# A two-block layer: gate sums of the matrix LSTM in nine matmuls, and the opening's loads in another order

## What is computed

```python
def _mlstm_feats(u, ib, fb):
    q, k, v, o, gates = _split_at(u, (ML_W, ML_W, ML_W, ML_W, 4 * ML_H))
    gates = gates.astype(jnp.float32).reshape(B, T, 2, 2, ML_H)
    ig = jnp.moveaxis(gates[:, :, :, 0] + ib, 1, -1)
    lf = jnp.moveaxis(jax.nn.log_sigmoid(gates[:, :, :, 1] + fb), 1, -1)
    return heads(q), heads(k) * ML_DH ** -0.5, heads(v), o, ig, lf

def _mlstm_scan(state, k, v, ig, lf, q, emit):
    b = jnp.cumsum(fc, axis=-1)
    dlog = jnp.where(tri, b[..., :, None] - b[..., None, :] + ic[..., None, :], -jnp.inf)
```

## Time and profile before

| | |
|---|---|
| median of 3 runs | 4479.27 us (4473.22 to 4482.85) |
| profiled execution | 4480.07 us, span 4478.3 us, mean granted TensorE clock 0.939 |
| TensorE (PE) busy | 4073.0 us, 91% |
| VectorE (DVE), ScalarE (ACT) busy | 2167.1 us, 1351.3 us |
| chain that ended last | PE 79%, DVE 12%, ACT 4%, issue 3%, DMA 1% |

### The profile page before, as it was taken

How to read it: one execution, slowest core, us unless ns; L and a number is a source line. 1 busy time by engine, 2 the same in 40 slices (tenths; PEclk the granted TensorE clock), 3 DMA queues, 4 the chain that set the end, 5 groups by cost and what they waited for, 6 DMA issues and landing times.

```text
span 4478.3 us, 70218 instructions
## 1 busy us (share of the span) xinstructions
PE 4073.0 (91%) x30400; PEld 3249.6 (73%) x30400; DVE 2167.1 (48%) x2920; ACT 1351.3 (30%) x1913; POOL 156.9 (4%) x197
## 2 busy tenths in 40 slices
PE   7987968877999999999978899999999987899998
PEld 4755768874767887888666578887888666578887
DVE  4756467753334445335555453335334646444335
ACT  4144243312324223222322432223222312433222
POOL 0000012220000000000000000000000001000000
PEclk8898979987999999999988899999999988889999
DMA  6111000015342223333200123332333100113331
GB/s 233 47 38 47 10 2 3 3 50 190 107 139 79 94 94 94 94 95 93 67 3 22 45 62 107 91 99 86 98 94 104 58 11 23 45 48 108 85 94 66
DMA packets 319381, 328.42 MB, mean 73 GB/s; under 512 B 10080, under 2 KB 243600, under 8 KB 318048
## 3 DMA queue, kind: packets, MB, share of 16 engines
q1 hardware_dynamic: 312144, 287.53, 20.9%
q0 software_dynamic: 6928, 36.40, 2.2%
HBM read 315.51 MB, written 8.39 MB: 72 GB/s over the span
## 4 chain that ended last, share of the span: by engine, by line
PE 79%; DVE 12%; ACT 4%; issue 3%; DMA 1%; POOL 0%; DVEq 0%; ACTq 0%; SPq 0%; POOLq 0%
PE psum L246 78%; DVE ring L300 3%; DVE ring L331 2%; DVE arena L300 2%; PE psum L253 2%; DVE arena L311 1%; ACT arena L350 1%; ACT ring L350 1%; DMA ring<-in_w_ada 1%; ACT r L350 1%; DVE r L300 1%; DVE arena L307 1%; DVE arena L305 0%; DVE arena L331 0%; DVE arena L319 0%
## 5 line engine op out<-in xcount | busy, mean ns | idle before, releaser
L246 PE MATMUL psum<-r 128*128 128x512 f32 (+2 forms) x13008 | 2928.7, 387 | 87.3 <-DVE r L300 70.4
L246 PEld LDWEIGHTS psum<-r 128*128 128x128 f32 x13008 | 2370.3, 189 | 636.3 <-issue 62.4
L300 DVE TENSOR_TENSOR r<-ring,r 128x2048 fp32r<-128x2048 f32 (+2 forms) x261 | 574.9, 2203 | 404.2 <-ACT r L350 399.7
L350 ACT ACTIVATE r<-ring 128x2048 fp32r<-128x2048 f32 (+2 forms) x261 | 479.2, 1836 | 401.5 <-PE psum L246 341.6
L350 ACT ACTIVATE arena<-psum 128x512 f32<-128x512 f32 (+6 forms) x472 | 258.9, 549 | 1125.1 <-PE psum L246 1045.8
L246 PE MATMUL psum<-arena 64*64 64x64 f32 (+18 forms) x2420 | 405.3, 335 | 56.0 <-DVE arena L300 29.8
L246 PE MATMUL psum<-ring 64*64 64x64 f32 (+4 forms) x8608 | 350.6, 236 | 86.2 <-ACT ring L350 34.5
L300 DVE TENSOR_TENSOR arena<-arena,psum 128x512 f32<-128x512 f32 (+4 forms) x220 | 129.9, 590 | 612.5 <-PE psum L246 559.5
L246 PEld LDWEIGHTS psum<-arena 128*128 128x128 f32 (+9 forms) x2420 | 261.2, 182 | 188.2 <-issue 112.9
L246 PEld LDWEIGHTS psum<-ring 64*64 64x64 f32 (+3 forms) x8608 | 289.6, 145 | 127.9 <-issue 48.3
L311 DVE SCALAR_TENSOR_TENSOR arena<-arena 128x512 f32<-128x512 f32 (+4 forms) x316 | 266.7, 844 | 117.9 <-ACT arena L350 107.0
(11 more groups left out here) (92 smaller groups left out, 1387.4 us busy)
## 6 DMA issues: line engine op xcount, KB each, us to landing
ring<-in_ffa_w_in SPq DMA_DIRECT2D x88, 512.0 KB, 5.2
ring<-in_ffb_w_in SPq DMA_DIRECT2D x88, 512.0 KB, 5.2
ring<-in_w_mlp SPq DMA_DIRECT2D x32, 1024.0 KB, 5.2
ring<-in_w_in SPq DMA_DIRECT2D x31, 1024.0 KB, 5.5
ring<-in_w_ada SPq DMA_DIRECT2D x24, 1024.0 KB, 5.5
ring<-in_mix_w_in SPq DMA_DIRECT2D x24, 1024.0 KB, 5.2
ring<-in_ffa_w_out SPq DMA_DIRECT2D x20, 1024.0 KB, 5.0
ring<-in_ffb_w_out SPq DMA_DIRECT2D x20, 1024.0 KB, 5.0
```

What stands on the lines that cost most here:

```text
L246: ins = self.raw.matmul(o, l, r, start=start, stop=stop, skip_group_check=True)
L300: self.done(self.raw and self.raw.tensor_tensor(o, a, b, f), keys)
L350: self.done(self.raw and self.raw.activation(o, i, f, scale=scale, bias=bias), keys)
```

## The change

Two things are changed. First, GpSimd waits, behind the four x tiles, until the sixth w_ada slab has been used, and only then issues ctx and the large constant tables. The norms of the two ctx tiles, on ScalarE and VectorE, move from the middle of the modulation rows to the end of the opening. Second, the sums of the gates are taken for all six tiles at once (nine matmuls: eight of 24 columns, one of 48), ahead of the rows; tiles that a direction doesn't need are computed too. VectorE makes the bias ahead of the rows, with 26 operations where there were 18, since the two neighbours that one copy read lie apart now.

```diff
@@ pool_first
         g.load(xtile(K, i), K.I["x"][0, 128 * i:128 * i + 128, :], "x", i)
+    g.wait_ge(*K.at("mod rows", 1, 0))
     for i in range(2):
         g.load(xtile(K, 4 + i), K.I["ctx"][0, 128 * i:128 * i + 128, :], "x", 4 + i)
     g.load(m.cst[:, 128:], K.I["consts"][:, 128:], "consts")
@@ act_first
     act_mod_rows(mod, K, 0, 1)
-    for i in (4, 5):
-        squares(i)
     act_mod_rows(mod, K, 1, 0, last=0)
...
         act_turned(a, K, "n1", 512, 0, f)
+    for i in (4, 5):
+        squares(i)
@@ dve_first
     dve_mod_rows(mod, K, 0, 1)
-    for i in (4, 5):
-        norm(i)
-    v.set(m.z[3], 0.0)
     dve_mod_rows(mod, K, 1, 0)
...
         dve_turned(v, K, "n1", 512, 0, f)
+    for i in (4, 5):
+        norm(i)
+    v.set(m.z[3], 0.0)
@@ pe_ml_rows
     t.wait_ge(*K.at("ml LF"))
+    o = t.take("ml sums")
+    for d in range(2):
+        lf, ig = m.LF[:, :, d, :], m.IG[:, :, d, :]
+        for x, mat in enumerate((C["LS128"], C["nUI128"]) if d == 0 else (C["US128"], C["nLI128"])):
+            p = view(o[:, 48 * d + 24 * x:48 * d + 24 * x + 24], [4, 6], [1, 4])
+            t.mm(p, mat, lf, True, False)
+            t.mm(p, C["ident"], ig, False, True)
+    t.mm(o[:, 96:144], C["ones"], view(m.LF, [1, 48]), True, True, ("ml sums",))
     for d in range(2):
         for x, X in enumerate((m.LF, m.IG)):
...
-    o = t.take("ml sums")
-    for d in range(2):
-        for x, tile in enumerate(SEQ_[d]):
-            lf, ig, c = m.LF[:, tile, d, :], m.IG[:, tile, d, :], 72 * d
-            if x < 5:
-                p = o[:, c + 8 * x:c + 8 * x + 4]
-                t.mm(p, C["LS128" if d == 0 else "US128"], lf, True, False)
-                t.mm(p, C["ident"], ig, False, True)
-            if 0 < x < 5:
-                t.mm(o[:, c + 44 + 4 * x:c + 48 + 4 * x], C["ones"], lf, True, True)
-            if x > 1:
-                p = o[:, c + 8 * x - 4:c + 8 * x]
-                t.mm(p, C["nUI128" if d == 0 else "nLI128"], lf, True, False)
-                t.mm(p, C["ident"], ig, False, True, ("ml sums",))
@@ dve_ml_in
     taps(conv, 9)
+    dve_ml_bias(v, K)
     dve_ml_rows(v, K)
     E.ahead()
-    dve_ml_bias(v, K)
     taps(conv, 18)
@@ dve_ml_bias
-        c, first = 72 * d, 18 * d
-        v.copy(m.bias[:, first, :], pv[:, c:c + 4])
-        last = first
+        P, D, T = ([pv[:, c + n * x:c + n * x + 4] for x in SEQ_[d]] for c, n in ((48 * d, 4), (48 * d + 24, 4), (96 + 4 * d, 8)))
+        last = first = 18 * d
+        v.copy(m.bias[:, first, :], P[0])
         for x in range(2, 6):
-            o = m.bias[:, first:first + x - 1, :]
-            v.tt(o, m.bias[:, last:last + x - 1, :], view(pv[:, c + 40 + 4 * x:c + 44 + 4 * x], [0, x - 1], [1, 4]), ADD)
-            v.copy(m.bias[:, first + x - 1:first + x + 1, :], view(pv[:, c + 8 * x - 8:c + 8 * x], [4, 2], [1, 4]),
-                   ("ml bias sb",))
+            v.tt(m.bias[:, first:first + x - 1, :], m.bias[:, last:last + x - 1, :], view(T[x - 1], [0, x - 1], [1, 4]), ADD)
+            v.copy(m.bias[:, first + x - 1, :], P[x - 1])
+            v.copy(m.bias[:, first + x, :], D[x], ("ml bias sb",))
             last, first = first, first + x + 1
```

## The result

The changed kernel takes 4443.45 us (median of 4 runs, 4441.4 to 4445.02) against 4476.25 us for the kernel before, timed beside it (4 runs): a ratio of 0.9925, 95% interval 0.9908 to 0.9943. Timed again in two later sessions it gave 4446.79 (ratio 0.993, 0.9918 to 0.9943) and 4446.95 us (0.9929, 0.9911 to 0.9948). The profiled execution took 4445.02 us with a span of 4443.2, against 4480.07 and 4478.3: 35.05 us less.

What follows compares the result with a forecast made beforehand. TensorE, busy 91% of the span, was taken as the bound, waiting for w_ada slabs and a bank held behind the sums. 8 us (9 - 1) plus 20.8 off 4479.3 gave 4451, range 4443 to 4463.

Steps and rivals of the forecast that it cites:

- w_ada first, 9 us (TensorE through at 35): Opening: with ctx and tables held back, TensorE finishes w_ada at 35 instead of 43.93, 9 us earlier (8 to 10).
- w_in's first split at 43, with two us of cover left: Opening: first w_in slab lands near 41; ScalarE splits it at 43 instead of 52.14, leaving two us to spare.
- Rival A: Opening: slab 7 or w_in's first slab waits out the 3.4 MB; the w_ada gain becomes 0, time 4458; chance 0.13.
- The rule of the Trainium skill: DMA queues: an engine drains a packet of each queue in turn, so large packets take the bandwidth.
- the argument against part one: Opening: w_in's first slab, in smaller pieces, crawls while tables run; the jam moves from slabs 3 to 5 onto slab 7 and w_in.
- Squares, 1.0 us: Opening: ctx's moved squares delay the split of w_in's second slab, costing 1.0 us (0 to 2).
- Sums, 1.8 us, and 3.5 idle: Matrix LSTM: nine products take 1.8 us instead of 15.17; TensorE then idles some 3.5 us before the eighth row group.
- k and v, 9.9 + 13.9 = 23.8 us: Matrix LSTM: k features take 9.9 us, then v's 60 matmuls 13.9 at 2.4 GHz, without a wait between.
- Rival B, the clock: Matrix LSTM: low clock lasts through k and v keeps 16.48 us; gain 10.8 instead of 20.8, time 4460; chance 0.11.
- C: Stages from 280 us on: clock falls come elsewhere and the kernel gets slower, 4488; chance 0.04.
- D: Matrix LSTM: VectorE with its 124 taps is the bound and TensorE waits there, so nothing arrives; about 4477; chance 0.04.
- The sum of 28.8 us: Total gain: 8 us from the opening plus 20.8 from the gate sums through the v features.

Runs made afterwards that it cites:

- What part two left: Changed kernel with the nine sums matmuls behind the eight row groups again and VectorE's bias between row copies and scans: 4442.97 us, ratio 0.9931.

## Why the prediction was right or wrong

The forecast was 4451, the time 4443.45: inside the range (4443 to 4463) by half a us, some 7 us below the likeliest, and outside the forecast's own bounds (4444 to 4461). The gain up to the first exponential was forecast rightly, in nearly all of its terms; the step from there to the time of the whole kernel failed.

- **w_ada first, 9 us (TensorE through at 35).** 34.25, 9.7 us. Slabs 2 and 3 were used at 17.0 and 19.7 (landing expected at 16.4 and 19.0), slab 5 done at 27.
- **w_in's first split at 43, with two us of cover left.** It came at 43.12, by two errors that cancel, which is luck. The turn of part 1 ran at the higher clock, so ScalarE was ready at 41.2; and the slab came at 43.1, not at 41. The traffic's length was about right (9 us, 8.4 forecast), its place was not: ctx was issued at 27.36, but GpSimd's queue moved nothing of it until 31, and was through at 40 where 38 was forecast. The cover wasn't left over but overspent by 1.95 us. Rival A was there, then, in small, and the tables' traffic was its cause, as the run that held them longer shows. What the lateness costs depends on ScalarE: in "What part two left", with the same opening, the turn ran at the low clock, ScalarE was ready later, and the wait was 0.23 us for a split at 43.02.
- **The rule of the Trainium skill (DMA: Bandwidth & Descriptors, on arbitration).** The trace agrees, if the profile's pieces are taken for the packets of that rule. In the changed kernel the queues moved, from 30 to 31, 33 to 34 and 35 to 40 us:

```profile
q1 hardware_dynamic: 350, 0.37, 110.1%
...
q0 software_dynamic: 84, 0.32, 79.0%
q1 hardware_dynamic: 84, 0.09, 24.2%
...
q0 software_dynamic: 115, 2.07, 97.4%
q1 hardware_dynamic: 115, 0.12, 6.8%
```

  Alone, SyncE's queue moves 350 pieces of w_in in 1 us. Beside ctx (pieces of 4 KB) it moves one of its 1 KB pieces for each of ctx's, and beside the tables (18 KB) too: 0.12 MB in 5 us, 5% of the bytes. So w_in did crawl, as the argument against part one had it. What it left out is the price. The crawl ends with the tables, at 40, and w_in was wanted only at 41.2, so 1.95 us of waiting were all that it cost.
- **Squares, 1.0 us.** 0.58 us of idle TensorE in the profile, and that wait is gone when the splits go first.
- **Sums, 1.8 us, and 3.5 idle.** 6.57 us for the sums and seven row groups against 1.8 + 4.6; idle 3.43. The bias took from 163.67 to the first row copy at 168.8, 26 operations at the forecast 0.197 us each.
- **k and v, 9.9 + 13.9 = 23.8 us.** 24.08, and 22.62 to 24.86 in other profiles of the same kernel.
- **Rival B, the clock.** It did fall between the rows and k, in four of the five profiles with the sums ahead of the rows (k and v in 24.08 to 24.86 us, against 22.62 in the fifth), but for 3 to 5 us of the k features and not for the whole of k and v. **C and D** got nothing: VectorE's taps were never waited for.

The sum of 28.8 us was measured as 28.71 at the first exponential (8.35 for the forecast 8, and 20.36 for 20.8). **What failed is the step behind it.** The prediction puts the stages from there on at nothing ("what is won there should be kept") and allows 4 us for them ("medians wander by 4 more"). They took 6.4 us less in the changed kernel's profile than in that of before, and 9.2 us less in one profile of before than in the other, with no edit between. The base was off as well: the 4479.27 from which I counted was the median of three, where four runs gave 4476.25 and later medians of before were 4475 to 4478. Of the 7 us that the forecast missed, 3 are the base and 4 are the stages behind. Over its 11 runs the changed kernel's median is 4445.9, some 31 us below before: 2 us more than the sum, which isn't told apart from chance.

## What to carry to other kernels

A bank, a slot or a tile that is freed by a cheap operation is held by whatever stands ahead of that operation in its engine's queue: of 21 us at the sums, moving one line won 10.8, without taking one matmul away. Loads that are wanted late should be issued behind those wanted early; making them smaller changes how the two queues share the bandwidth, but not the bytes that stand in the way. A change of under 1% is better read from an event shortly behind it than from the time of the whole kernel.

## What the runs showed of the hardware

The low clock follows small work too, not only idle time. In the kernel before, the windows from 176 to 180 and 180 to 184 us, with TensorE busy throughout on the matmuls of 4 columns, are (the clock is the third figure from the end):

```profile
176.00:180.00 4.00, 4.00 (x24) 4.00 (x24) 3.83 (x4) 0.00 (x0) 0.00 (x0) 0.59 0.00 0
180.00:184.00 4.00, 4.00 (x21) 4.00 (x20) 2.38 (x4) 0.00 (x0) 0.00 (x0) 0.50 0.00 0
```

With the 3.4 us idle taken out, TensorE busy all through from 164.31 with 18 small matmuls and then k, it was near 0.50 from 167 to 170, in the midst of large matmuls. With nearly the same order of work it did not fall at all in another kernel (108 matmuls in 22.60 us against 24.15); no run here shows why.

While both DMA queues had work, they took turns piece by piece, one to one, in each of three windows with different sizes. SyncE's queue against GpSimd's: 109 to 106 with pieces of 2 against 17 KB (before, 20 to 25 us), 361 to 362 with 2 against 3.3 KB (tables in nine pieces), 115 to 115 with 1 against 18 KB (changed, 35 to 40 us). The bytes follow the sizes: 11%, 38% and 5% for SyncE's queue.
